# Attention blocks taken two at a time, and the modulation dots spread over fixed steps, in a hybrid encoder step

## The chip, the core and the metric

The kernel runs on one core of a Trainium2 chip. The metric is the device time of one execution in microseconds (us), as a median of several runs. The core has a matrix engine (PE, TensorE, which writes to PSUM banks), VectorE (DVE), ScalarE (ACT), GpSimd (POOL) and SyncE (SP, which here only issues DMA transfers). Each engine works through its own list of instructions in order; they meet at semaphores. Code such as `pe.wait_ge(x, n)` holds PE's list until the semaphore x has reached n.

## What is computed

One layer of a streaming encoder, on 1024 prompt frames and 64 sample frames (T = 1088 tokens in all), in float32. Cut to what matters here:

```python
mod = silu(c) @ w_ada + b_ada                    # shift, scale and gate vectors from the conditioning
h = modulate(rmsnorm(x, ln1), sh1, sc1)
rq, rk, rv, rg, aq, ak, av = split_in(h @ w_in)   # two groups of heads out of one projection
ret_o = retention(rq, rk, rv, rg)                 # 4 heads x 128, a carried state per head
att_o = band_attention(aq, ak, av, sinks)         # 8 query heads, 2 kv heads x 64, window 128, ALiBi, sinks
x = x + g1 * (concat(ret_o, att_o) @ w_out)
h2 = modulate(rmsnorm(x, ln2), sh2, sc2)
x = x + g2 * conv_ffn(h2)                         # gated MLP with a causal convolution of width 3
y = modulate(rmsnorm(x, normf), shf, scf)
```

The attention adds a table of distances and a mask to the scores, takes the row maximum (with the sink), exponentiates, divides by the sum and weighs the values. The retention takes blocks of 128 tokens: scores times a decay table, plus the query times the state carried so far, and a new state.

## The kernel before

**Stages.** A start (normalisation of x and the first three projection units, until about 88 us of the trace), then four "heads" j = 0 to 3 (88 to 450 us), then the output projection, the up projection with the convolution, and the down projection. The change touches the heads alone.

**Units, passes and steps.** Activations lie with features on partitions, tokens along the free axis. A unit is one 128-column tile of `w_in`: it is multiplied with all tokens in three chunks of 364, 362 and 362 columns (PSUM banks 0, 1, 2), and each chunk takes three passes of 8 matmuls (weights and activations are split in a high and a low part). Head j has the units rq, rk, rv, rg and the next head's aq, so 5 x 9 passes; the last head has 4 units and then, in `first_out_unit`, the first unit of the output projection in place of the fifth. After each pass `unit` (line 1922 issues the matmuls) calls `between`, which puts small matmuls for attention and retention in. Pass i of unit p ends in **step** 9p + i: 45 steps a head, with 8 unit matmuls between two steps. A **stretch** s is three steps (3s to 3s + 2); the lists of DVE and ACT are written out by stretches.

**Attention of head j** has 9 query blocks b: 8 of 128 tokens and the last of 64. Four parts on PE and three elsewhere follow one another for a block:
- `scores` (PE, L2006): for both kv groups, keys against queries, into banks 3 and 4; in step 3b.
- `mask_and_max` (DVE, L1460 to L1465): adds the table, takes the maximum, and prepares the exponent's bias, into `prob` and `soft`, which hold two blocks; in stretch b.
- `exps` (ACT, L835, L837), then `normalise` (DVE, L1473 to L1476) in stretch b + 1.
- `transpose_prob` (PE, L2021): four transposes into bank 5, in step 3b + 4; `copy_prob_t` (ACT, L845).
- `weigh_values` (PE, L2036): into bank 6, in step 3b + 6, behind the scores of block b + 2; `copy_att_out` (ACT, L854).

**Retention of head j** has 9 blocks as well. `RET_PE_STEP` gives the PE steps 28, 30, 31, ..., 38. In its k-th entry PE issues `block_scores(k)` (L2051 to L2053, banks 3 or 4) and then `block_output(k - 1)` (L2070 to L2073, banks 6 and 5), which waits for DVE's `take_block(k - 1)` and `next_state(k - 2)`. DVE does `retention(k)` = `take_block(k)` (L1490 to L1492) and `next_state(k - 1)` (L1505) in the stretch that holds the step: k = 0 in stretch 9; 1, 2, 3 in 10; 4, 5, 6 in 11; the rest in 12. In the last head `mix_lo` (L1518) follows most of them on DVE and prepares the low parts for the output projection; POOL does some of these too (L1261).

**Modulation dots.** Each head computes 8 rows of `w_ada` against the conditioning: `ada_dots` (L1352) is two dots of 1024 elements by 128 partitions on DVE, with both operands and the result in SBUF. It waits for a row tile in `ada_w` (two places, so the load of tile i + 2 waits, in SP's list, until the dots of tile i are done). Dots i = 0 to 7 stand at the end of stretches 1 to 8; then `add_ada_bias` (L1358).

**POOL** splits a unit's weights in their low part (L1203, 128 x 1024) when ACT has made the high part (L730), once at the end of each unit. In unit 0 it also scales rq for the retention (`decay_q`, L1227 and L1230), and at the start of a head it finishes the retention output of the head before (`gate_ret`, L1241 and L1244). Ahead of that DVE has three reciprocals (L1559), 7 us together, between two heads.

## Time and profile before

| | |
|---|---|
| median of 3 runs | 1325.32 us (1324.27 to 1325.89) |
| the profiled execution | 1324.34 us, span 1322.5 us |
| busy: PE, weight loads | 1254.9 us (95%), 1182.0 us (89%) |
| busy: DVE, ACT, POOL | 840.2 us (64%), 517.5 us (39%), 520.5 us (39%) |
| mean granted TensorE clock | 0.984 of full speed |
| chain that ended last, by engine | PE 68%, DVE 12%, POOL 6%, issue 5%, DMA 5%, ACT 2% |
| unit matmuls of the heads, L1922 | 1368, 256.5 us busy |

A line of the trace's timeline gives start, duration, engine, source line, operation, result <- operands, and a count where several were merged; in brackets stands idle time of the engine ahead of it, and what ended it. Starts are counted from the start of the span. A matmul's duration overlaps with the next one's; its cost is the distance of two starts. Float32 matmuls are issued in two passes, so that two of them show as x4.

### The profile page before, as it was taken

To read this page: it belongs to the slowest core of one execution; us is meant where nothing else is said; L and a number is where in the kernel's file an instruction comes from. 1 tells how busy PE (TensorE), PEld (TensorE's weight loads), DVE (VectorE), ACT (ScalarE), POOL (GpSimd) and SP (SyncE) were. 2 spreads that over 40 slices of the span, in tenths; PEclk is the share of its full clock that TensorE was granted. 3 is DMA by queue.
4 is the path that set the end of the run, shared out by engine and by line. 5 is a ranking of instruction groups with operands and counts; after the bars stand their busy time and mean duration, and the time that the engine had idled before them with its cause. 6 is when DMAs were issued, how large, how long until landed. Compare 5 with 4: busy or idle time off the path is not lost.

```text
span 1322.5 us, 22445 instructions
## 1 busy us (share of the span) xinstructions
PE 1254.9 (95%) x8537; PEld 1182.0 (89%) x8537; DVE 840.2 (64%) x1503; ACT 517.5 (39%) x1029; POOL 520.5 (39%) x313
## 2 busy tenths in 40 slices
PE   5999999999999999779999999999999999999995
PEld 3568988988989899779999999999999999999995
DVE  6988477396496637995666666666665468663305
ACT  4454345344345513543333333433333323333422
POOL 0012131031232514544353534435352577775760
PEclk9999999999999899899999999999999999999998
DMA  9413032222233412103223232222322898686971
GB/s 363 177 58 125 25 121 79 81 80 87 74 112 103 149 60 99 58 32 132 99 100 115 92 124 99 100 99 100 115 94 83 324 367 289 238 310 213 332 258 46
DMA packets 74392, 185.55 MB, mean 140 GB/s; under 512 B 7424, under 2 KB 39744, under 8 KB 74048
## 3 DMA queue, kind: packets, MB, share of 16 engines
q1 hardware_dynamic: 72640, 183.63, 38.9%
q8 instruction: 59, 0.97, 0.3%
q10 hardware_dynamic: 1664, 0.72, 0.2%
q14 instruction: 29, 0.24, 0.1%
HBM read 150.14 MB, written 34.19 MB: 139 GB/s over the span
## 4 chain that ended last, share of the span: by engine, by line
PE 68%; DVE 12%; POOL 6%; issue 5%; DMA 5%; ACT 2%; SPq 1%; DVEq 0%; ACTq 0%; POOLq 0%
PE bank L2189 33%; PE bank L1922 14%; PE bank L2229 9%; PE bank L2165 5%; DMA w_raw<-in_w_units 3%; POOL w_extra L1315 2%; POOL w_more L1315 2%; PE bank L2036 2%; DVE std L1559 1%; PE bank L2006 1%; PE bank L2021 1%; DVE ada_out L1352 1%; DVE act_hl L1406 1%; POOL w_hl L1315 1%; POOL w_hl L1276 1%
## 5 line engine op out<-in xcount | busy, mean ns | idle before, releaser
L1922 PE MATMUL bank<-act_hl,w_hl 128*128 128x362 f32 (+1 forms) x1368 | 256.5, 336 | 1.3 <-DVE act_hl L1406 1.3
L1922 PEld LDWEIGHTS bank<-act_hl,w_hl 128*128 128x128 f32 x1368 | 223.3, 188 | 10.6 <-issue 8.3
L1203 POOL TENSOR_TENSOR w_hl<-w_raw,w_hl 128x1024 fp32r<-128x1024 f32 x21 | 51.3, 2444 | 332.5 <-ACT w_hl L730 332.5
L2229 PE MATMUL bank<-u_hl,w_more 128*128 128x362 f32 (+1 forms) x672 | 116.3, 332 | 2.6 <-POOL w_more L1315 2.3
L2189 PE MATMUL bank<-x_blocks_a,w_hl 128*128 128x272 f32 x864 | 114.0, 291 | 4.9 <-issue 4.9
L2229 PEld LDWEIGHTS bank<-u_hl,w_more 128*128 128x128 f32 x672 | 113.5, 191 | 3.3 <-POOL w_more L1315 2.6
L2189 PEld LDWEIGHTS bank<-x_blocks_a,w_hl 128*128 128x128 f32 x864 | 111.6, 191 | 5.3 <-issue 5.1
L2189 PE MATMUL bank<-x_blocks_a,w_ext 128*128 128x272 f32 x840 | 110.1, 290 | 4.3 <-DVE prod_sb L1664 2.4
L2189 PE MATMUL bank<-x_blocks_b,w_hl 128*128 128x272 f32 x864 | 112.7, 288 | 1.6 <-ACT x_blocks_b L1013 1.3
L2189 PEld LDWEIGHTS bank<-x_blocks_b,w_hl 128*128 128x128 f32 x864 | 109.8, 188 | 2.4 <-DVE up_b L1669 1.3
L2189 PEld LDWEIGHTS bank<-x_blocks_a,w_ext 128*128 128x128 f32 x840 | 107.5, 190 | 5.0 <-issue 2.6
L2189 PE MATMUL bank<-x_blocks_b,w_ext 128*128 128x272 f32 x840 | 108.3, 287 | 0.0
L2189 PEld LDWEIGHTS bank<-x_blocks_b,w_ext 128*128 128x128 f32 x840 | 106.2, 188 | 0.0
L1315 POOL TENSOR_TENSOR w_more<-w_raw,w_more 128x1024 fp32r<-128x1024 f32 x28 | 76.0, 2734 | 49.6 <-ACT w_more L1103 49.6
L2229 PE MATMUL bank<-u_hl,w_hl 128*128 128x362 f32 (+1 forms) x480 | 83.6, 330 | 3.1 <-POOL w_hl L1315 2.8
L1276 POOL TENSOR_TENSOR w_ext<-w_raw,w_ext 128x512 fp32r<-128x512 f32 x40 | 52.9, 1340 | 83.2 <-ACT w_ext L990 83.2
L1276 POOL TENSOR_TENSOR w_hl<-w_raw,w_hl 128x512 fp32r<-128x512 f32 x40 | 52.3, 1323 | 81.2 <-ACT w_hl L990 81.2
L2229 PEld LDWEIGHTS bank<-u_hl,w_hl 128*128 128x128 f32 x480 | 80.1, 189 | 4.3 <-POOL w_hl L1315 3.4
L2229 PE MATMUL bank<-u_hl,w_extra 128*128 128x362 f32 (+1 forms) x432 | 74.0, 330 | 1.9 <-POOL w_extra L1315 1.9
L2229 PEld LDWEIGHTS bank<-u_hl,w_extra 128*128 128x128 f32 x432 | 72.0, 188 | 3.0 <-POOL w_extra L1315 2.8
L1315 POOL TENSOR_TENSOR w_hl<-w_raw,w_hl 128x1024 fp32r<-128x1024 f32 x20 | 52.8, 2654 | 33.6 <-ACT w_hl L1103 33.6
L2165 PE MATMUL bank<-act_hl,w_hl 128*128 128x272 f32 x480 | 64.1, 297 | 2.0 <-POOL w_hl L1269 2.0
(233 smaller groups left out, 2277.7 us busy)
## 6 DMA issues: line engine op xcount, KB each, us to landing
w_raw<-in_w_units SPq DMA_DIRECT2D x139, 512.0 KB, 4.5
ada_w<-in_w_ada_t SPq DMA_DIRECT2D x36, 512.0 KB, 3.6
u_hl<-u_dram SPq DMA_DIRECT2D x44, 362.0 KB, 5.5
u_dram<-acc SPq DMA_DIRECT2D x22, 544.0 KB, 2.7
u_dram<-up_b SPq DMA_DIRECT2D x22, 544.0 KB, 2.7
ada_d<-in_w_ada_t SPq DMA_DIRECT2D x16, 512.0 KB, 5.7
u_hl<-u_dram SPq DMA_DIRECT2D x22, 364.0 KB, 7.3
xm<-in_x_t SPq DMA_DIRECT2D x2, 1448.0 KB, 13.8
```

What stands on the lines that cost most here:

```text
L1203: pool.tensor_tensor(w_hl[:, slot, 1], w_raw[:, slot], w_hl[:, slot, 0].bitcast(F32), ALU.subtract).then_inc(wl_ready, 1)
L1276: pool.tensor_tensor(w_block(q)[:, 1], a_source(f, i), w_block(q)[:, 0].bitcast(F32), ALU.subtract).then_inc(bl_ready, 1)
L1315: pool.tensor_tensor(w_down(q)[:, 1], w_raw[:, q % 3], w_down(q)[:, 0].bitcast(F32), ALU.subtract).then_inc(dl_ready, 1)
L1352: dve.tensor_tensor_reduce(out, ada_place[place], silu_c[:, s], 1.0, 0.0, ALU.mult, ALU.add, mod_part[:, part, s:s + 1]).then_inc(ada_used, 1)
L1406: dve.tensor_tensor(act_hl[:, 1, k, :], xm[:, k, :], act_hl[:, 0, k, :].bitcast(F32), ALU.subtract).then_inc(lo_ready, 1)
L1559: dve.reciprocal(std[:, c, 0:n], std[:, c, 0:n]).then_inc(inv_ready, 1)
L1922: ins = pe.matmul(bank[c][:, 0:m], w_hl[:, slot, w, k, :], act_hl[:, x, k, a:a + m], start=(pas == 0 and i == 0), stop=(pas == 2 and i == ...
L2006: ins = pe.matmul(bank[3 + g][0:n, 0:kn], aq[h, t:t + n], ak[h, kb[0][0]:kb[0][0] + kn], start=True, stop=True)
L2036: ins = pe.matmul(bank[6][h, 0:n], av_tok[0:k[1], k[3], h], prob_t[0:k[1], r, g, i, 0:n], start=(i == 0), stop=(i == len(kb) - 1))
L2165: ins = pe.matmul(bank[r % 3][:, 0:HC], w_of[:, w, k, :], act_hl[:, x, k, HC * n:HC * n + HC], start=(pas == i == 0), stop=(pas == 2 and i ...
L2189: ins = pe.matmul(n[:, 0:HC], w_block(q)[:, w, P * k:P * (k + 1)], x_half(h)[:, i, x, k, :], start=(first and pas == k == 0), stop=(pas == ...
L2229: ins = pe.matmul(bank[o][:, 0:m], w_down(q)[:, w, o, :], u_hl[:, q % U_RING, x, 0:m], start=(f == pas == 0), stop=(f == FT - 1 and pas == 2))
```

## The change

- Attention's PE parts move to fixed steps, two blocks at a time: scores of (0, 1), (2, 3), (4, 5), (6, 7), (8) in steps 0, 6, 12, 18, 24; transposes in steps 6, 12, 18, 24, 28; values of (0, 1), (2, 3), (4, 5) in steps 12, 18, 24, of (6, 7) in step 28 and of (8) in step 30. Within a step PE issues values, scores, transposes, then retention, in this order.
- The two blocks of a pair use two halves of banks 3, 4 and 6, and banks 5 and 7 for the transposes. `qk_ready` and `pv_ready` are raised once for a pair, by 2. Bank 7 is free when the norm of the head before is done, so the wait for `std_ready` moves from the first values to the first odd transpose.
- DVE masks a pair in stretches 0, 2, 4, 6, 8 and normalises it in stretches 1, 3, 5, 7, 9. The masking of a pair waits for the scores of both blocks.
- The dots stand at the end of stretches 1, 2, 4, 6, 8, 9, 10, 11, behind the retention parts of that stretch; the bias follows the last. ACT's list follows the same tables, values first, then transposes, then exponents.
- Numbers and shapes of all matmuls, DVE, ACT and POOL operations and of all transfers stay as they are.

```diff
--- before.py
+++ after.py
@@ -840,7 +840,7 @@
 
                 qn, r, kb = BLOCKS[b][1], b % 2, keys_of(b)
                 act.wait_ge(pt_ready, NB * j + b + 1)
-                src = bank[5][:, :].rearrange("p (g k q) -> p g k q", g=2, k=2)
+                src = bank[5 + 2 * r][:, :].rearrange("p (g k q) -> p g k q", g=2, k=2)
                 if b < NB - 1:
                     ins = act.activation(prob_t[:, r, :, 0:len(kb), :], src[:, :, 0:len(kb), :], ACT.Copy)
                 else:
@@ -851,7 +851,8 @@
             def copy_att_out(j, b):
                 t, n = BLOCKS[b]
                 act.wait_ge(pv_ready, NB * j + b + 1)
-                act.activation(xm[:, 4 + j, t:t + n], bank[6][:, 0:n], ACT.Copy).then_inc(pv_copied, 1)
+                at = P * (b % 2)
+                act.activation(xm[:, 4 + j, t:t + n], bank[6][:, at:at + n], ACT.Copy).then_inc(pv_copied, 1)
 
             def copy_ret_out(j, b):
                 t, n = BLOCKS[b]
@@ -895,12 +896,13 @@
                         if s == 14:
                             ret_squares(j, (2,))
                             ret_roots(j, (0, 1))
-                        if 2 <= s <= NB + 1:
-                            copy_att_out(j, s - 2)
-                        if s < NB:
-                            exps(j, s)
-                        if 1 <= s <= NB:
-                            copy_prob_t(j, s - 1)
+                        for step in range(3 * s, 3 * s + 3):
+                            for b in ATT_PV_AT.get(step, ()):
+                                copy_att_out(j, b)
+                            for b in ATT_PT_AT.get(step, ()):
+                                copy_prob_t(j, b)
+                            for b in ATT_QK_AT.get(step, ()):
+                                exps(j, b)
                         if mixing and c == 0:
                             split_weights(UNIT_OUT + 1, [UNIT_OUT + 1])
                         for step in (3 * s, 3 * s + 1):
@@ -1457,7 +1459,7 @@
                 dve.wait_ge(qk_ready, NB * j + b + 1)
                 seal_waits(dve)
                 for g in range(2):
-                    ins = dve.tensor_tensor_reduce(prob[0:qn, r, g, 0:kn], bank[3 + g][0:qn, 0:kn],
+                    ins = dve.tensor_tensor_reduce(prob[0:qn, r, g, 0:kn], bank[3 + g][0:qn, 256 * r:256 * r + kn],
                                                    att_tab[0:qn, g, kb[0][2]:kb[0][2] + kn], 1.0, sink_sb[0:qn, g:g + 1],
                                                    ALU.add, ALU.max, soft[0:qn, r, 0, g:g + 1])
                 chain(ins, j)
@@ -1536,19 +1538,20 @@
                         next_state(j, k - 1)
 
                 for s in range(3 * (N_HEAD - last)):
-                    if 1 <= s <= NB:
-                        normalise(j, s - 1)
-                    if s < NB:
-                        mask_and_max(j, s)
-                    if 1 <= s <= 8:
-                        ada_dots(16 + s - 1 + 8 * j, 2 + (s - 1) // 2 + 1 + 4 * j, (s - 1) % 2, s - 1)
-                    if s == NB:
-                        chain(add_ada_bias(16 + 8 * j, 8, 16 + 8 * j + 8), j)
+                    for b in ATT_QK_AT.get(3 * s, ()):
+                        mask_and_max(j, b)
+                    for b in ATT_QK_AT.get(3 * s - 3, ()):
+                        normalise(j, b)
                     for k in range(NB + 1):
                         if RET_PE_STEP[k] // 3 == s:
                             retention(k)
                             if last and k in MIX_LO_AFTER:
                                 mix_lo(*MIX_LO_AFTER[k])
+                    if s in ADA_AT:
+                        i = ADA_AT.index(s)
+                        ada_dots(16 + i + 8 * j, 2 + i // 2 + 1 + 4 * j, i % 2, i)
+                    if s == ADA_AT[-1]:
+                        chain(add_ada_bias(16 + 8 * j, 8, 16 + 8 * j + 8), j)
                 for k in range(7, NB + 1) if last else ():
                     retention(k)
                     mix_lo(*MIX_LO_AFTER[k])
@@ -1997,45 +2000,48 @@
                 if b == 0:
                     pe.wait_ge(av_tok_ready, 3)
                     pe.wait_ge(cache_loaded, 32)
-                else:
+                elif b % 2 == 0:
                     pe.wait_ge(masked_ready, NB * j + b)
                     if b == NB - 1:
                         seal_waits(pe)
+                at = 256 * (b % 2)
                 for g in range(2):
                     h = slice(64 * g, 64 * g + 64)
-                    ins = pe.matmul(bank[3 + g][0:n, 0:kn], aq[h, t:t + n], ak[h, kb[0][0]:kb[0][0] + kn],
+                    ins = pe.matmul(bank[3 + g][0:n, at:at + kn], aq[h, t:t + n], ak[h, kb[0][0]:kb[0][0] + kn],
                                     start=True, stop=True)
-                ins.then_inc(qk_ready, 1)
+                if b % 2 or b == NB - 1:
+                    ins.then_inc(qk_ready, 1 + b % 2)
 
             def transpose_prob(j, b):
                 n, r, kb = BLOCKS[b][1], b % 2, keys_of(b)
                 pe.wait_ge(prob_ready, NB * j + b + 1)
-                if b > 0:
-                    pe.wait_ge(pt_copied, NB * j + b)
+                if b >= 2:
+                    pe.wait_ge(pt_copied, NB * j + b - 1)
+                if b == 1:
+
+                    pe.wait_ge(std_ready, 3 + 3 * j)
                 if b == NB - 1:
                     seal_waits(pe)
                 for g in range(2):
                     at = 0
                     for i, k in enumerate(kb):
                         col = P * (2 * g + i)
-                        ins = pe.transpose(bank[5][0:k[1], col:col + n], prob[0:n, r, g, at:at + k[1]], ident[0:n, 0:n])
+                        ins = pe.transpose(bank[5 + 2 * r][0:k[1], col:col + n], prob[0:n, r, g, at:at + k[1]], ident[0:n, 0:n])
                         at += k[1]
                 ins.then_inc(pt_ready, 1)
 
             def weigh_values(j, b):
                 n, r, kb = BLOCKS[b][1], b % 2, keys_of(b)
                 pe.wait_ge(pt_copied, NB * j + b + 1)
-                if b > 0:
+                if b % 2 == 0 and b > 0:
                     pe.wait_ge(pv_copied, NB * j + b)
-                else:
-
-                    pe.wait_ge(std_ready, 3 + 3 * j)
                 for g in range(2):
                     h = slice(64 * g, 64 * g + 64)
                     for i, k in enumerate(kb):
-                        ins = pe.matmul(bank[6][h, 0:n], av_tok[0:k[1], k[3], h], prob_t[0:k[1], r, g, i, 0:n],
+                        ins = pe.matmul(bank[6][h, P * r:P * r + n], av_tok[0:k[1], k[3], h], prob_t[0:k[1], r, g, i, 0:n],
                                         start=(i == 0), stop=(i == len(kb) - 1))
-                ins.then_inc(pv_ready, 1)
+                if b % 2 or b == NB - 1:
+                    ins.then_inc(pv_ready, 1 + b % 2)
 
             def block_scores(j, b):
 
@@ -2080,13 +2086,12 @@
                 def between(p):
                     def steps(i):
                         s = 9 * p + i
-                        b = s // 3
-                        if s % 3 == 0 and b < NB:
+                        for b in ATT_PV_AT.get(s, ()):
+                            weigh_values(j, b)
+                        for b in ATT_QK_AT.get(s, ()):
                             scores(j, b)
-                        if s % 3 == 1 and 1 <= b <= NB:
-                            transpose_prob(j, b - 1)
-                        if s % 3 == 0 and 2 <= b <= NB + 1:
-                            weigh_values(j, b - 2)
+                        for b in ATT_PT_AT.get(s, ()):
+                            transpose_prob(j, b)
                         if s in RET_PE_STEP:
                             k = RET_PE_STEP.index(s)
                             if k < NB:
@@ -2268,6 +2273,12 @@
 
 MIX_ORDER = [4, 5, 6, 7, 0, 1, 2, 3]
 
+ATT_PV_AT = {12: (0, 1), 18: (2, 3), 24: (4, 5), 28: (6, 7), 30: (8,)}
+ATT_QK_AT = {0: (0, 1), 6: (2, 3), 12: (4, 5), 18: (6, 7), 24: (8,)}
+ATT_PT_AT = {6: (0, 1), 12: (2, 3), 18: (4, 5), 24: (6, 7), 28: (8,)}
+
+ADA_AT = (1, 2, 4, 6, 8, 9, 10, 11)
+
 RET_PE_STEP = [28] + list(range(30, 39))
 
 RET_SUM_STEP = [{41: (0, 1), 43: (2,)}, {40: (0, 1), 42: (2,)}]
```

## Rows read from the trace of the kernel before

**Rows 1.** The page, first part: engine, busy time, share of the span, instructions.

```profile
PE 1254.9 (95%) x8537; PEld 1182.0 (89%) x8537; DVE 840.2 (64%) x1503; ACT 517.5 (39%) x1029; POOL 520.5 (39%) x313
```

**Rows 2.** Chain of waits, a period of three steps in head 1: start, us, what.

```profile
205.36 0.63 PE bank L2006 x4
205.99 0.59 PE bank L2036 x8
206.59 1.53 PE bank L1922 x8
208.11 0.44 PE bank L2021 x4
208.55 2.65 PE bank L1922 x16
```

**Rows 3.** Chain of waits, step 28 of head 1, behind the transposes of block 8.

```profile
231.05 0.26 PE bank L2051
```

**Rows 4.** Timeline of PE: first scores and last transposes of heads 0, 2, 3.

```profile
87.74 0.49 PE L2006 MATMUL bank<-ak,aq 64*128 64x128 f32 x4
140.00 0.45 PE L2021 MATMUL bank<-ident,prob 64*128 64x64 f32 x4
267.34 0.49 PE L2006 MATMUL bank<-ak,aq 64*128 64x128 f32 x4
321.24 0.45 PE L2021 MATMUL bank<-ident,prob 64*128 64x64 f32 x4
357.97 0.49 PE L2006 MATMUL bank<-ak,aq 64*128 64x128 f32 x4
411.30 0.45 PE L2021 MATMUL bank<-ident,prob 64*128 64x64 f32 x4
```

**Rows 5.** Timeline of DVE in head 1: first mask, and one tile's dots.

```profile
179.88 0.25 DVE L1460 CUSTOM_DVE_ANT_0 prob<-bank,att_tab,sink_sb 128x128 f32<-128x128 f32 x1
...
185.62 1.23 DVE L1352 CUSTOM_DVE_ANT_0 ada_out<-ada_w,silu_c 128x1024 bf16<-128x1024 f32 x1
...
188.19 0.16 DVE L1473 TENSOR_TENSOR rden<-soft 128x2 f32<-128x2 f32 x1
```

**Rows 6.** Timeline of DVE and POOL, two places where both work on SBUF.

```profile
193.27 2.74 DVE L1476 TENSOR_SCALAR prob<-prob,rden 128x256 f32<-128x256 f32 x2
193.35 2.51 POOL L1203 TENSOR_TENSOR w_hl<-w_raw,w_hl 128x1024 fp32r<-128x1024 f32 x1 [7.90 <-ACT w_hl L730]
...
376.94 2.41 POOL L1227 TENSOR_TENSOR acc<-rq,rtab 128x1024 f32<-128x1024 f32 x1
376.99 3.43 DVE L1352 CUSTOM_DVE_ANT_0 ada_out<-ada_w,silu_c 128x1024 bf16<-128x1024 f32 x1
```

**Rows 7.** Timeline of all engines around steps 35 to 37 of head 1.

```profile
247.37 0.27 PE L2051 MATMUL bank<-ident,rk 128*128 128x128 f32 x1
...
248.75 0.34 DVE L1505 SCALAR_TENSOR_TENSOR state<-state,rtab,bank 128x128 f32<-128x128 f32 x1
...
250.09 2.38 POOL L1203 TENSOR_TENSOR w_hl<-w_raw,w_hl 128x1024 fp32r<-128x1024 f32 x1 [18.97 <-ACT w_hl L730]
...
250.52 0.35 DVE L1490 TENSOR_SCALAR k_tok<-bank,rtab 128x128 f32<-128x128 f32 x1 [1.44 <-PE bank L2053]
...
252.82 0.49 PE L2070 MATMUL bank<-s_dec,v_tok 128*128 128x128 f32 x2
```

**Rows 8.** Timeline of POOL, DVE and PE in the last head, steps 33 and 34.

```profile
422.71 2.58 POOL L1261 TENSOR_TENSOR act_hl<-xm,act_hl 128x362 fp32r<-128x362 f32 x2 [5.25 <-ACT act_hl L883]
...
424.39 0.34 DVE L1490 TENSOR_SCALAR k_tok<-bank,rtab 128x128 f32<-128x128 f32 x1
...
425.96 0.39 PE L2070 MATMUL bank<-s_dec,v_tok 128*128 128x128 f32 x2
```

**Rows 9.** Windows in the output projection: length, busy of each engine (x instructions), granted clock.

```profile
451.83:458.66 6.83, 6.83 (x47) 6.83 (x46) 1.22 (x3) 4.58 (x8) 6.26 (x3) 0.82 0.56 167
458.66:465.49 6.83, 6.83 (x56) 6.83 (x55) 6.04 (x5) 1.92 (x3) 5.40 (x3) 1.00 0.40 140
```

## The prediction

> **What bounds the kernel now.** I read the page first: PE is busy for 95% of the span [rows 1], so a gain has to come out of PE's own list, and a loss out of waits that are put into it. Then the chain of waits inside a head. In the steady part it lies on PE alone [rows 2]: scores 0.63 us, values 0.59, then 8 unit matmuls in 1.53, transposes 0.44, then 16 unit matmuls in 2.65. Sixteen in 2.65 is 0.166 each, so 8 should take 1.33. The 8 that come back from the values take 0.20 more, the 16 behind the transposes nothing. Attention's small matmuls use half of the array's rows (scores, 64*128) or columns (values, 128*64), the unit and the transposes all of it; the 0.20 is the price of a return to the full array.
>
> Next I compare the heads. From the first scores to the last transposes PE takes 52.26 us in head 0, 53.90 in head 2 and 53.33 in head 3 [rows 4], with the same work; head 1 is like head 2. The excess, 2 x 1.64 + 1.07 = 4.35 us, is PE waiting for DVE, which is still busy with the reciprocals of the head before and masks its first block only 3 us into the head [rows 5].
>
> **Part 1: pairs on PE.** No matmul goes away. Of returns to the full array from scores or values there are ten in a head now (scores in step 0, the eight steps 3 to 24, values in step 27); steps 28 and 30 end in retention. Afterwards only step 0 has one, since every later step ends in transposes or retention. Nine returns x 0.20 x 4 heads = 7.2 us off PE, all on the path. Values followed by scores, and scores followed by transposes, become new transitions, about 8 a head. The nearest row is the first retention transpose behind the half-size ones of block 8, 0.26 [rows 3] against 0.11 (a quarter of 0.44): 0.15 each, 4.8 us if all cost that. On the other side, if second blocks also shed what is lost inside a group (values are 0.59, where four times 0.11 would do), 0.15 x 8 x 4 = 4.8 us more go. So the gain is 2.4 to 12 us; I take 7.2, because the times in rows 2 already contain the change from one half-array shape to another.
>
> The Trainium skill, TensorEngine Tiling (Array Packing), Key Properties, says that a change of tiling mode drains the engine. By that rule only the number of changes counts, three for each block now and three for each pair afterwards, which would put the gain near the upper bound.
>
> **Part 2: waits at the head's start.** DVE starts the first mask at 179.88 [rows 5], 3.2 us behind PE's first scores. Two masks, exponents and two normalisations end about 6.5 us later, at 186.4; the first transposes now come in step 6, some 48 x 0.166 + 1.3 = 9.3 us into the head plus the scores of a pair (1.3), near 187.5. The 4.35 us go.
>
> **Part 3: a normalisation beside POOL.** Normalisation of (2, 3) is queued on DVE behind the dots of tile 1. On ACT the exponents of block 3 precede the split of the unit's weights, so POOL begins its 2.5 us split and the 2.4 + 0.3 us of `decay_q` at about the moment at which the normalisation begins. Rows 6 show what then happens: two L1476, 0.61 us elsewhere, took 2.74 beside the split. Counted through, block 3 is normalised 1.6 us after PE wants its transposes in step 12 (nominally 198.7 in head 1's time). In head 0, with no reciprocals ahead, 0.1. Sum 0.1 + 3 x 1.6 = 4.9 us; the ends are 0 (DVE slips in ahead of POOL) and 7.
>
> **Part 4: dots among the retention.** A tile's dots take 188.19 - 185.62 = 2.57 us of DVE [rows 5]. From step 30 on, PE steps follow each other by 2.44 us (247.37 for step 35), and in each `block_output` waits for DVE's retention part of the step before. What is late:
> - Tile 5, at the end of stretch 9, has the 4.6 us to step 30's retention: nothing, in the last head 0.3.
> - Tile 6, between retention(3) and retention(4): DVE had 1.4 us idle a step and PE needs the state one step later. 2.57 fits but for 0.1 in heads 0 to 2.
> - Tile 7, behind retention(6), whose last operation ends at 249.09 [rows 7]. First dot to about 250.3. POOL's split is ready at 250.09 and takes the SBUF in between, for 2.4 us, to 252.7. The second dot ends at 254.0, the bias at 254.25, then retention(7) needs about 1.0 until the state is written: 255.25. PE's L2070 of step 37 stood at 252.82 and waits for that state: 2.4 us. Nothing else can run on PE, since its unit matmuls are queued behind. Three heads: 3 x (2.4 + 0.1) = 7.5 us. That a dot waits for a whole POOL operation is shown once at full length: 3.43 instead of 1.23, beside L1227 [rows 6].
> - In the last head DVE also has `mix_lo`. Retention(4) starts at 424.39 and ends 1.0 later, 0.6 ahead of PE's 425.96 [rows 8]. Tile 6 comes before it, and waits until 425.3 for POOL's L1261 as well: 0.9 + 2.57 - 0.6 = 2.9 us late. Tile 7 meets the next pair of L1261 in the same way, with the bias on top: 3.1. With tile 5's 0.3 that is 6.3 us; without any POOL wait it would be 4.1.
>
> The skill's page SBUF — State Buffer, Who interferes with whom, says that a DVE instruction with two SBUF inputs and a GpSimd one that reads SBUF exclude each other for the whole instruction, the first one winning. By that rule the second dot of tile 7 is blocked to the end of the split; rows 6 agree. Without it the three heads would lose 0.35 us each instead of 2.5.
>
> **Costed at nothing.** The tile loads are issued later, since each waits for the dots two tiles back, and two unit loads queue behind them on SP; they land some 4 us after issue and are used 10 us or more later, except tile 7 (issued after tile 5's dots, about 12 us ahead). If that cover were gone, a unit's split would be late by the difference. The evacuations that ACT does behind two blocks of exponents have a whole unit (17 us) of slack. The moved `std_ready` wait is satisfied 15 us before.
>
> **Clock.** After PE's waits around 446 to 451 us the granted clock was half (1.2 GHz of 2.4) until about 454: 47 matmuls in 6.83 us against 56 in the next 6.83 [rows 9], 1.1 us lost on the part at half. Five new waits of 2.4 to 3.1 us are nearly as long as those. An estimate: half of them bring a stretch at half clock like that one, 2.5 x 1.1 = 2.7 us; ends 0 and 8.
>
> **The sum**, on the profiled execution of 1324.34 us: - 7.2 - 4.35 + 4.9 + 7.5 + 6.3 + 2.7 = +9.85, so 1334.2 us. The median of before is 1325.32, so against it the change is +8.9 us or 0.7%. The stages behind the heads are taken as unchanged, shifted in time.
>
> **The rivals.**
> - *DVE's SBUF work is not held up* (ends faster). In rows 7, L1490 ran in its usual 0.35 under the split. If dots and normalisations do so as well, Part 3 is 0, tile 7 costs 0.25 and tile 6 0.1 in three heads (1.05), and the last head 4.1. 1324.34 - 11.55 + 1.05 + 4.1 = 1317.9. Against: L1490 reads a PSUM bank, the dots do not. It decides at the second dot of tile 7: if that ends before 252 in head 1's time, this rival holds. 0.12.
> - *PE sheds more than I count*: the upper bound of Part 1 (12) with all waits as forecast, Part 3 nought and no clock loss: 1324.34 - 12 - 4.35 + 7.5 + 6.3 = 1321.8; with one of these at its middle, 1324. 0.16, half of it faster by more than 0.2%.
> - *DVE becomes the bound of the heads*: transitions at 0.15 each (gain 2.4), Part 3 at 7, and clock losses of 8: 1324.34 - 2.4 - 4.35 + 7 + 7.5 + 6.3 + 8 = 1346. For it: DVE is 64% busy and its retention parts sit one step ahead of PE. 0.07.
> - *The change does not do what it says*: waits inside a merged step break the pair up, so that no return is saved, 1341. Since the scores of a step need only masks of the pair before, I see no such wait but that of Part 3. 0.05.
> - The forecast, 1328 to 1341: 0.60.
>
> **How the numbers follow.** About 0.2% (2.7 us) is what a measurement of this kernel can tell from no change. Faster: 0.12 + 0.08 = 0.20. Same (1322.7 to 1328): 0.08 of the second rival and 0.05 at the forecast's lower edge, 0.13. Slower: 0.67. The range leaves out half of the first rival and the outer part of the third: 1319 to 1342.
>
> **What would show it.** Right: in a steady pair step PE's values, scores and transposes take about 3.3 us with no extra in the unit matmuls behind; the first transposes of heads 1 to 3 wait for nothing; an idle PE of 2.4 us ahead of L2070 in step 37 of heads 0 to 2, and a second L1352 of about 3.4 us under L1203; two waits near 3 us in the last head. Wrong: a second dot of 1.23 us in stretch 11, PE waits for `mix_lo` in the last head's output unit, or a new wait for a weight split.

## The result and the profile after

The changed kernel takes 1335.27 us (median of 4 runs, 1332.67 to 1339.13) against 1325.61 us beside it (1324.27 to 1326.34): a ratio of 1.0074, 95% interval 1.0050 to 1.0097. It is slower by 9.7 us. The profiled execution took 1339.13 us with a span of 1337.4. The page's first part, in the columns of [rows 1]:

```profile
PE 1251.9 (94%) x8537; PEld 1190.4 (89%) x8537; DVE 854.2 (64%) x1503; ACT 517.0 (39%) x1029; POOL 522.2 (39%) x313
```

PE is busy 3 us less than in [rows 1] and the span is 15 us longer, so PE waits more. Which engine it waits for is told by the table of PE's waits (line <- releaser: us in total, times, longest). Two groups grew in the heads: `block_output` (L2076), which has no such group before, and the transposes (L2029), which before waited 2.4 us in all, 5 times. The wait of the last head's output unit for `mix_lo` is as before (3.2 us in all against 3.0).

```profile
PE bank L2076 <- DVE state L1507: 11.8, 5, 2.8
PE bank L2029 <- DVE prob L1478: 5.2, 10, 0.8
```

Windows cut at the first scores of each head, with the last one up to the output projection, show where the time goes: length, PE busy, PEld, DVE, ACT, POOL, then the granted clock. First before, then after:

```profile
87.74:176.72 88.98, 88.98 (x593) 79.79 (x592) 54.14 (x161) 37.34 (x102) 15.55 (x7) 1.00 0.25 84
176.72:267.34 90.62, 89.53 (x594) 79.73 (x593) 58.41 (x163) 37.57 (x103) 20.23 (x13) 1.00 0.24 82
267.34:357.97 90.63, 89.53 (x593) 79.74 (x593) 58.40 (x163) 37.57 (x103) 20.23 (x13) 1.00 0.23 82
357.97:451.70 93.73, 89.92 (x585) 79.74 (x585) 71.31 (x185) 47.21 (x127) 33.63 (x26) 0.98 0.33 107
```

```profile
87.34:178.58 91.24, 88.27 (x593) 81.87 (x592) 58.21 (x161) 36.99 (x102) 14.62 (x7) 0.98 0.25 87
178.58:270.73 92.15, 88.38 (x594) 81.92 (x593) 62.85 (x163) 37.59 (x103) 20.16 (x13) 0.98 0.23 80
270.73:363.07 92.34, 88.55 (x594) 82.08 (x593) 62.93 (x163) 37.59 (x103) 20.16 (x13) 0.98 0.23 80
363.07:463.00 99.93, 90.31 (x585) 82.76 (x585) 76.08 (x185) 46.65 (x127) 35.49 (x26) 0.95 0.30 101
```

Heads 0 to 2 are 2.26, 1.53 and 1.71 us longer. The last one, up to the first matmul of the output projection, grew from 93.74 to 100.0 us. In heads 0 to 2 PE is busy about one microsecond less, yet 3 to 4 us of each are now idle, and the clock column is 0.98 where it was 1.00, so the busy time holds some work at a lower clock.

**The gain.** The chain of waits in a steady merged step, which answers to [rows 2]:

```profile
209.69 1.07 PE bank L2041 x16
210.76 1.06 PE bank L2010 x8
211.83 1.02 PE bank L2029 x8
212.85 3.17 PE bank L1925 x19
```

Values, scores and transposes of two blocks take 1.07 + 1.06 + 1.02 = 3.15 us, and the 19 unit matmuls behind them 3.17, 0.167 each, no extra. Before it was 2 x (0.63 + 0.59 + 0.20 + 0.44) = 3.72 [rows 2].

**The loss.** The largest part is in the retention. DVE, POOL and PE in step 37 of head 1, which answers to [rows 7]:

```profile
248.62 1.22 DVE L1354 CUSTOM_DVE_ANT_0 ada_out<-ada_w,silu_c 128x1024 bf16<-128x1024 f32 x1
...
249.71 2.38 POOL L1205 TENSOR_TENSOR w_hl<-w_raw,w_hl 128x1024 fp32r<-128x1024 f32 x1 [19.81 <-ACT w_hl L730]
...
250.04 3.13 DVE L1354 CUSTOM_DVE_ANT_0 ada_w<-ada_w,silu_c 128x1024 f32<-128x1024 f32 x1 [0.19 <-DVE mod_part L1354]
...
254.66 0.74 PE L2076 MATMUL bank<-s_dec,v_tok 128*128 128x128 f32 x2 [2.12 <-DVE state L1507]
```

The second dot of tile 7 takes 3.13 us in place of 1.22 and ends 1.1 us behind POOL's split (249.71 + 2.38 = 252.09). The retention part behind it is late, and PE stands for 2.12 us. Then comes what the windows behind that wait show (same columns as above):

```profile
252.50:254.70 2.20, 0.08 (x2) 0.07 (x1) 1.99 (x8) 0.00 (x0) 0.00 (x0) 1.00 0.00 0
254.70:258.10 3.40, 3.40 (x13) 3.40 (x14) 0.79 (x4) 0.28 (x1) 0.00 (x0) 0.50 0.00 0
258.10:261.50 3.40, 3.40 (x20) 2.92 (x20) 0.35 (x1) 1.61 (x4) 0.00 (x0) 1.00 0.08 22
```

With PE idle for 2.1 us, the granted clock falls to half (1.2 of 2.4 GHz) for the next 3.4 us: 13 matmuls there, 20 in the same length after it. All five long waits of the heads (step 37 in heads 0 to 2, steps 34 and 37 in the last) are followed by such a stretch in this execution. That is not so in every one: see the run with the placement alone.

A smaller part is in the attention. Steps 12 and 28 of head 1, where a normalisation (L1478) meets POOL's split and the transposes behind it wait (in step 12 twice, 0.83 and 0.39 us):

```profile
195.20 2.41 POOL L1205 TENSOR_TENSOR w_hl<-w_raw,w_hl 128x1024 fp32r<-128x1024 f32 x1 [7.85 <-ACT w_hl L730]
195.59 4.53 DVE L1478 TENSOR_SCALAR prob<-prob,rden 128x256 f32<-128x256 f32 x2
...
200.17 0.66 PE L2029 MATMUL bank<-ident,prob 128*128 128x128 f32 x4 [0.83 <-DVE prob L1478]
...
227.30 2.71 DVE L1478 TENSOR_SCALAR prob<-prob,rden 64x192 f32<-64x192 f32 x2
...
230.16 0.42 PE L2029 MATMUL bank<-ident,prob 64*128 64x64 f32 x4 [0.43 <-DVE prob L1478]
```

### The profile page after: what moved, and what is told of

Its sections match the earlier page's. It is cut to its first block, busy times and chain, and to the rows that moved or that the text cites. A ratio compares the mean times of both kernels' runs of the same rounds, so it can differ in the third digit from the quotient of the medians.

```text
span 1337.4 us, 22424 instructions
## 1 busy us (share of the span) xinstructions
PE 1251.9 (94%) x8537; PEld 1190.4 (89%) x8537; DVE 854.2 (64%) x1503; ACT 517.0 (39%) x1029; POOL 522.2 (39%) x313
## 4 chain that ended last, share of the span: by engine, by line
PE 64%; DVE 16%; issue 7%; POOL 5%; DMA 4%; ACT 2%; SPq 2%; DVEq 0%; ACTq 0%; POOLq 0%
PE bank L2194 32%; PE bank L2234 11%; PE bank L1925 10%; PE bank L2170 5%; DMA w_raw<-in_w_units 2%; DVE prob L1478 2%; DVE ada_out L1354 2%; POOL w_extra L1317 1%; DVE std L1562 1%; PE bank L2041 1%; DVE prob L1462 1%; PE bank L2029 1%; POOL w_hl L1317 1%; POOL w_hl L1278 1%; DMA ada_d<-in_w_ada_t 1%
## 5 line engine op out<-in xcount | busy, mean ns | idle before, releaser
L1925 PE MATMUL bank<-act_hl,w_hl 128*128 128x362 f32 (+1 forms) x1368 | 246.4, 336 | 1.1 <-POOL w_hl L1205 1.1
L1925 PEld LDWEIGHTS bank<-act_hl,w_hl 128*128 128x128 f32 x1368 | 228.3, 191 | 4.4 <-issue 2.7
L1205 POOL TENSOR_TENSOR w_hl<-w_raw,w_hl 128x1024 fp32r<-128x1024 f32 x21 | 54.4, 2591 | 334.7 <-ACT w_hl L730 334.7
L1317 POOL TENSOR_TENSOR w_hl<-w_raw,w_hl 128x1024 fp32r<-128x1024 f32 x20 | 52.7, 2648 | 36.0 <-ACT w_hl L1105 36.0
```

Of the source, the lines that this page charges most:

```text
L1205: pool.tensor_tensor(w_hl[:, slot, 1], w_raw[:, slot], w_hl[:, slot, 0].bitcast(F32), ALU.subtract).then_inc(wl_ready, 1)
L1317: pool.tensor_tensor(w_down(q)[:, 1], w_raw[:, q % 3], w_down(q)[:, 0].bitcast(F32), ALU.subtract).then_inc(dl_ready, 1)
L1925: ins = pe.matmul(bank[c][:, 0:m], w_hl[:, slot, w, k, :], act_hl[:, x, k, a:a + m], start=(pas == 0 and i == 0), stop=(pas == 2 and i == ...
```

## The experiments

The theory: the pairs on PE are a gain of about 14 us with the heads' starts, and everything lost comes from where the dots stand, by three mechanisms: the dots' own length, DVE's stop behind POOL's work in SBUF, and the half clock behind PE's long waits. The rivals: the loss comes with the pairs; POOL only happens to run beside the dots; the half clock has another cause.

**Dots put back to stretches 1 to 8.**

```diff
-ADA_AT = (1, 2, 4, 6, 8, 9, 10, 11)
+ADA_AT = (1, 2, 3, 4, 5, 6, 7, 8)
```

> The changed kernel with the dots of a head put back to the ends of stretches 1 to 8; the attention in pairs stays. It tells the two halves of the change apart. Theory (the loss is made by the dots that stand among the retention, and the pairs alone are a gain): the waits of 2.2 us in step 37 of heads 0 to 2 and of 2.7 and 2.9 us in the last head go, and so do the stretches at half clock behind them; what stays is the wait of step 12 (0.6 + 1.45 + 1.5 + 1.25 = 4.7 us) and the 0.46 us of step 28. By the traces: 1325.3 - 9.6 (pairs) - 4.35 (heads' start) + 4.7 + 1.4 = 1317.4; counted from the changed kernel's 1335.3 it would be 1314. So 1314 to 1318. Rival (most of the loss comes with the pairs, as more waits in the merged steps): 1326 or more.

Measured: 1321.26 us, ratio to before 0.9966 (0.9956 to 0.9977). The change's sign flips with the dots alone, so the rival falls; but the time is 3 us above the expected range. PE's waits in L2076 are gone. In their place there is one of 1.30, 1.30 and 1.35 us in step 28 of heads 0 to 2 (0.51 in the last), which the expectation had at 0.46. Head 1:

```profile
225.77 2.37 POOL L1205 TENSOR_TENSOR w_hl<-w_raw,w_hl 128x1024 fp32r<-128x1024 f32 x1 [15.81 <-ACT w_hl L730]
226.06 2.11 DVE L1360 TENSOR_TENSOR mod<-mod_part,b_ada_sb 128x16 f32 x1 [0.17 <-DVE mod_part L1354]
...
228.59 0.54 DVE L1478 TENSOR_SCALAR prob<-prob,rden 64x192 f32<-64x192 f32 x2
229.28 0.42 PE L2029 MATMUL bank<-ident,prob 64*128 64x64 f32 x4 [1.30 <-DVE prob L1478]
```

The bias (L1360) follows the last tile, and it met POOL's split: 2.11 us for an operation of 16 columns that takes 0.17 elsewhere. The normalisation behind it was late. The four waits of step 28 are 4.5 us in place of the 1.4 expected, which is 3.1 of the 3.9 us that the time lies above the sum.

**Last tile out of stretch 11.**

```diff
-ADA_AT = (1, 2, 4, 6, 8, 9, 10, 11)
+ADA_AT = (1, 2, 4, 5, 6, 8, 9, 10)
```

> The changed kernel, dots at the ends of stretches 1, 2, 4, 5, 6, 8, 9, 10: no tile in stretch 11 any more. Theory: in heads 0 to 2 the 2.2 us wait of step 37 goes with its stretch at half clock (about 1.7 us each), and in the last head the wait of step 37 (2.9 us and its 1.7); the wait of step 34 of the last head stays at 2.7. 1335.3 - 3 x 3.9 - 4.6 = 1319. Rival (the clock falls have another cause and stay): 1335.3 - 3 x 2.2 - 2.9 = 1325.8. Rival (the wait only moves to the step behind the tile, now in stretch 10, since DVE is full there too): 1333 to 1336.

Measured: 1322.11 us (ratio 0.9974, 0.9964 to 0.9984), 13.2 us below the changed kernel, where 16 were expected. Heads 0 to 2 took 87.64, 88.52 and 88.54 us, which is 3.6 to 3.8 less than in the changed kernel, where 3.9 were expected; the last head came down by 4.0, to 96.0. That makes 15.0 us in the profiles, of the 16.3 that the expectation adds up to. In the medians another 1.8 are missing; the sizes had been read from the changed kernel's profiled run, which was its slowest. The rival in which the clock falls stay (1325.8) is 3.7 us too high, and the granted clock of heads 0 and 1 is 1.00; the one in which the wait only moves is out: tile 7 costs 0.29 us in stretch 10.

**POOL's split cut short.**

```diff
-pool.tensor_tensor(w_hl[:, slot, 1], w_raw[:, slot], w_hl[:, slot, 0].bitcast(F32),
+pool.tensor_tensor(w_hl[:, slot, 1, 0:kt], w_raw[:, slot, 0:kt], w_hl[:, slot, 0, 0:kt].bitcast(F32),
...
-split_weights(head_unit(j, p) + 2, [head_unit(0, p) + 2])
+split_weights(head_unit(j, p) + 2, [head_unit(0, p) + 2], 1 if p in (2, 3) else KT)
```

> The changed kernel, but in heads 0 to 2 POOL's subtraction that makes the low part of the weights covers only the first 128 of its 1024 columns for two of the five units of a head (those whose split falls beside step 28 and beside step 37); the rest of these low parts is left out of the computation. DVE's, ACT's and PE's lists are as they were. Theory (the second dot of tile 7 and the normalisation of block 8 wait for the end of the split in SBUF): the second dot falls from 3.1 to 1.25 us, the wait of step 37 from 2.2 to about 0.3 us, the 0.46 us of step 28 go, and with them the half clock behind step 37: 1335.3 - 3 x (1.9 + 0.46 + 1.7) = 1323. The last head stays. Rival (DVE is late by the length of its own work, POOL only happens to run beside it): both waits and the time stay, 1334 to 1336. If the waits go but not the half clock: 1328.

Measured: 1327.06 us (ratio to before 1.0006, 0.9993 to 1.0019). Not one instruction of DVE or PE differs from the changed kernel, and the same place of head 1 now reads:

```profile
245.39 0.45 POOL L1205 TENSOR_TENSOR w_hl<-w_raw,w_hl 128x128 fp32r<-128x128 f32 x1 [21.25 <-ACT w_hl L730]
...
245.72 1.22 DVE L1354 CUSTOM_DVE_ANT_0 ada_w<-ada_w,silu_c 128x1024 f32<-128x1024 f32 x1 [0.19 <-DVE mod_part L1354]
...
248.44 0.46 PE L2076 MATMUL bank<-s_dec,v_tok 128*128 128x128 f32 x2 [0.25 <-DVE state L1507]
```

The dot is back at 1.22 us, the wait at 0.25, and step 28 waits for nothing. Heads 0 to 2 shrink by 3.9 us each (91.24, 92.15, 92.34 to 87.35, 88.28, 88.43), where 4.06 was forecast; the last head stays at 100.0. POOL is the cause, and the dots' own length leaves 0.25 us of 2.1. The median is 4 us above the expected 1323, though the heads of the profiles show the full 11.7 us: as in the run above, the sizes were read in the slowest run of the changed kernel and taken off its median.

**Waits filled with matmuls.**

```diff
+last = isinstance(j, int)
+if b == 7 or last and b == 4:
+    ...
+    for i in range(14 if last else 11):
+        k = ks[i % len(ks)]
+        pe.matmul(bank[7][:, 0:362], w_hl[:, slot, 0, k, :], act_hl[:, 0, k, lo:lo + 362],
+                  start=True, stop=True)
 pe.matmul(bank[6][:, 0:n], v_tok[0:n, r, :], s_dec[0:n, r, 0:n], start=True, stop=(b == 0))
```

> The changed kernel, with matmuls whose result nobody reads, into the free bank 7, ahead of the waiting block_output: 11 in step 37 of heads 0 to 2, 14 in steps 34 and 37 of the last head, 362 columns each. They fill most of PE's waits, which stay as long as they are. Theory (the half clock follows PE's idle time): the waits end when they did, but no half clock comes behind them: 5 x up to 1.7 us, 1335.3 - 5 to 8 = 1327 to 1330. Rival (the half clock comes from elsewhere, or returns as much as was saved): 1334 to 1337. If the fillers are longer than the waits, by their excess more.

Measured: 1329.77 us, 5.5 us less than the changed kernel, with 61 matmuls more. PE in head 1, and the windows of the filler and of the stretch behind it:

```profile
251.28 2.08 PE L2072 MATMUL bank<-act_hl,w_hl 128*128 128x362 f32 x11
...
253.47 0.46 PE L2084 MATMUL bank<-s_dec,v_tok 128*128 128x128 f32 x2
```

```profile
251.28:253.40 2.12, 2.08 (x13) 1.77 (x11) 1.91 (x8) 0.00 (x0) 0.00 (x0) 1.00 0.00 0
253.40:256.80 3.40, 3.33 (x21) 2.87 (x21) 0.90 (x4) 0.75 (x2) 0.00 (x0) 1.00 0.00 0
```

The output matmul of step 37 starts as late as before, and the clock behind it is 1.00 with 21 matmuls in 3.4 us; so it is behind all five filled waits. The mean granted clock of the ten runs is 0.985 to 0.987, where the four of the changed kernel have 0.980 to 0.984: where PE's idle time is filled, the half clock stays away. Heads 0 to 2 lose 1.43, 1.35 and 1.61 us, the last one 3.0 for its two waits: one stretch at half clock costs 1.5 us, five of them 7.4 in the profiles, 5.5 by the medians.

**The placement alone, on the kernel before** (in DVE's list of before, the last three lines of the loop over stretches as in the changed kernel; nothing else).

> The kernel before, with nothing changed but the place of the dots: ends of stretches 1, 2, 4, 6, 8, 9, 10, 11, behind the retention parts. Attention stays block by block. With the run that put the dots back, it tells whether the two halves of the change add up. Theory: the waits of steps 34 and 37 come as in the changed kernel, with their half clock: 3 x (0.1 + 2.2 + 1.7) + 2.7 + 2.9 + 3.4 = +21, less up to 2 us of the waits at the heads' start, as stretch 3 has no dots: 1344. The clock lost 2 to 3 us less in timed runs than in the profiled one, so 1340 to 1345. Rival (the waits need the pairs, which put two normalisations and two masks in a stretch): 1325 to 1330.

Measured: 1343.58 us (ratio 1.0140, 1.0118 to 1.0163), within the range of the theory. The waits do not need the pairs: PE stands for 2.16, 2.12 and 2.12 us in step 37 of heads 0 to 2 and for 2.55 and 2.87 in the last. The two halves add up: -10.2 and -4.35 us from pairs and heads' starts, +4.5 and +1.4 from the two waits that only pairs bring (steps 12 and 28; the sizes are in the table below) make -8.7, and from this run to the changed kernel it is 1335.27 - 1343.58 = -8.3.

The half clock, however, is not as the theory had it. Behind four of the five waits the granted clock stayed at 1.00 in the profiled execution. Head 0, the same place as in head 1 of the changed kernel:

```profile
164.25 0.46 PE L2071 MATMUL bank<-s_dec,v_tok 128*128 128x128 f32 x2 [2.16 <-DVE state L1505]
...
164.91 1.58 PE L1923 MATMUL bank<-act_hl,w_hl 128*128 128x364 f32 x8
```

The 8 unit matmuls take 1.58 us; in head 1 of the changed kernel, behind a wait of 2.12 us, they take 2.57. Only head 2 shows half clock, from 351.1 to 358.1 us, and is 3.0 us longer than head 1. So a wait of 2.1 to 2.9 us can bring half clock and need not; what decides it, these runs don't show. That the time was met all the same is luck in part: the waits at the heads' start did not shrink as forecast (0.70 to 0.92 us where 0.69 was), and 2.5 us of the profiled execution arose behind the heads.

**Dots between.**

```diff
 for b in ATT_QK_AT.get(3 * s - 3, ()):
     normalise(j, b)
+if s == 9:
+    ada_dots(16 + 6 + 8 * j, 2 + 3 + 1 + 4 * j, 0, 6)
...
-i = ADA_AT.index(s)
+i = (0, 1, 2, 3, 4, 5, 7)[ADA_AT.index(s)]
...
-ADA_AT = (1, 2, 4, 6, 8, 9, 10, 11)
+ADA_AT = (1, 3, 4, 5, 6, 7, 9)
```

> A version meant to keep the pairs' gain without the waits: attention in pairs as in the changed kernel; dots of tile 0 at the end of stretch 1, none in 2, tiles 1 to 5 at the ends of 3 to 7, none in 8, tile 6 in stretch 9 between the normalisation of block 8 and the first retention part, tile 7 at the end of stretch 9. Theory: with no dots in stretch 2 the normalisation of (2, 3) starts ahead of POOL's split, so the wait of step 12 goes; with none in 8 the normalisation of block 8 is in time; stretches 10 and 11 have retention alone. 1325.3 - 9.6 - 4.35 = 1311.4, range 1310 to 1314. Rival (two tiles in stretch 9 make the first retention part late): a wait ahead of step 30 of up to 2 us in each head, 1315 to 1319.

Measured: 1311.52 us (1309.93 to 1313.23), ratio to before 0.9891 (0.9877 to 0.9906). It beats both kernels, at the expected 1311.4. Its heads:

```profile
87.75:174.18 86.43, 86.43 (x594) 80.38 (x593) 54.24 (x161) 36.90 (x102) 17.21 (x7) 1.00 0.26 87
174.18:260.64 86.46, 86.46 (x594) 80.42 (x593) 61.07 (x163) 37.39 (x103) 21.70 (x13) 1.00 0.25 86
260.64:347.10 86.46, 86.46 (x594) 80.42 (x593) 61.08 (x163) 37.38 (x103) 21.71 (x13) 1.00 0.25 86
```

PE is never idle in three heads, and their clock column is 1.00. The rival's wait for the first retention part shows in the last head alone, 0.74 us. Yet the collision with POOL is still there; nobody waits behind it (head 1):

```profile
221.77 2.37 POOL L1205 TENSOR_TENSOR w_hl<-w_raw,w_hl 128x1024 fp32r<-128x1024 f32 x1 [15.28 <-ACT w_hl L730]
221.87 3.36 DVE L1354 CUSTOM_DVE_ANT_0 ada_w<-ada_w,silu_c 128x1024 f32<-128x1024 f32 x1 [0.19 <-DVE mod_part L1354]
225.16 0.34 DVE L1492 TENSOR_SCALAR k_tok<-bank,rtab 128x128 f32<-128x128 f32 x1
```

**One tile in stretch 8 in place of the middle of 9.** The edit: the two added lines go, and `ADA_AT = (1, 3, 4, 5, 6, 7, 8, 9)`.

> As the version with the dots between, but tile 6 at the end of stretch 8 in place of the middle of stretch 9 (stretch 2 stays empty, tile 7 stays at the end of 9). It tells which of the two moves removed which wait. Theory: the wait of step 12 stays away, since it hung on the dots in stretch 2; the wait of step 28 comes back, since the normalisation of block 8 then stands behind two sets of dots and starts beside POOL's split: 1.3 us in a head, as in the run with the dots early: 1311.5 + 4 x 1.3 = 1316.7. Rival (the wait of step 28 hangs on the sum of the dots up to there, which is 7 tiles here and 8 in that run): 1311 to 1313.

Measured: 1314.31 us (1312.53 to 1317.03), between the two expectations. Step 12 waits for nothing, step 28 for 0.66, 0.49 and 0.48 us in heads 0 to 2, which the rival did not have. That the place of each tile counts, and not how many came before, is shown by two other runs: the changed kernel has five tiles ahead of that normalisation and a wait of 0.43 us, the run with the dots between has six and no wait. But 0.5 us is not 1.3: here the bias stands in stretch 9, out of the way, and the normalisation itself meets the split (2.66 us at 222.40 in head 1, where POOL starts at 222.52). The forecast had carried the 1.3 over without it.

**Transposes first, and values and scores interleaved.** Both on the version with the dots between, where no wait disturbs PE.

```diff
+for b in ATT_PT_AT.get(s, ()) if s < 28 else ():
+    transpose_prob(j, b)
 for b in ATT_PV_AT.get(s, ()):
     weigh_values(j, b)
 for b in ATT_QK_AT.get(s, ()):
     scores(j, b)
```

> As the version with the dots between (run beside it), but in steps 6, 12, 18 and 24 PE issues transposes, then values, then scores, so that the unit follows half-size matmuls. The number of changes of shape in a step stays the same; what changes is that 4 steps a head end in half-size matmuls in place of transposes. By the prediction's step (0.20 us for a return to the unit from half-size matmuls, nothing from transposes): 4 x 4 x 0.20 = +3.2 us against the version beside it. Rival (every change of shape costs the same, wherever it stands): 0, within 0.5 us.

Measured: 1312.32 us against 1311.52, +0.8 in place of +3.2. The runs of the two versions overlap (1311.13 to 1313.57, 1309.93 to 1313.23), so 0.8 is hardly told from nothing, but well from 3.2. The chain of waits in step 18 of head 1:

```profile
203.97 0.87 PE bank L2031 x8
204.84 1.07 PE bank L2043 x16
205.92 1.06 PE bank L2012 x8
206.98 1.03 PE bank L1927 x5
```

Five unit matmuls take 1.03 behind the scores, 0.20 more than 5 x 0.166, as in [rows 2]. But the transposes cost 0.87 where they cost 1.02 behind scores. The return from half-size matmuls is paid either way: 0.20 at the unit, or 0.15 at the transposes. This step is 0.05 us longer in all. In step 6 of heads 1 to 3 there was 0.2 to 0.3 us more, with a gap between the transposes of the two blocks: they stand 1.1 us earlier in this order, and in head 1 DVE's normalisation of block 1 ends at 183.02, just ahead of its transposes at 183.15. In head 0, where it ends 3 us earlier, step 6 is 0.02 us longer.

```diff
+for i in range(2):
+    for b in ATT_PV_AT.get(s, ())[i:i + 1]:
+        weigh_values(j, b)
+    for b in ATT_QK_AT.get(s, ())[i:i + 1]:
+        scores(j, b)
```

> As the version with the dots between (run beside it), but in steps 12, 18 and 24 values and scores alternate (values b, scores b', values b + 1, scores b' + 1), which puts two more changes of shape in each of these steps, 24 in all; between half-size shapes only. Theory A (a change between two half-size shapes costs as much as a return to the full array, 0.20 us): +4.8 us against the version beside it. Theory B (only the return to the full array costs): +0 to 0.5 us.

Measured: 1314.94 us, +3.4. The same step:

```profile
204.83 0.59 PE bank L2043 x8
205.42 0.63 PE bank L2012 x4
206.06 0.59 PE bank L2043 x8
206.65 0.63 PE bank L2012 x4
207.28 1.02 PE bank L2031 x8
```

3.46 us in place of 3.15, for the same 32 matmuls: two more changes of shape cost 0.31 us, 0.155 each. So it is theory A, with a price three quarters as large. The expectation also counted one change too many a head: in step 24 there is only block 8 to score, which makes one more change and 0.11 us more (2.67 in place of 2.56). That is 5 a head, 20 in all, and 0.70 us longer heads 1 and 2 in the profiles. The blocks now cost exactly what they cost one by one (0.59 and 0.63, [rows 2]).

## Why the prediction was right, and where it was not

The predicted 1334.2 us stands against 1335.3. The sum, in the order of its terms; "found" is from the traces.

| term | forecast | found | from |
|---|---|---|---|
| pairs on PE | -7.2 | -10.2 | head 0, 88.98 to 86.43 with the dots between, x 4 |
| heads' starts | -4.35 | -4.35 | heads 1 and 2 no longer than head 0 (86.46, 86.43) |
| step 12 | +4.9 | +4.5 | 0.46 + 1.36 + 1.53 + 1.15: how much later PE is in step 18 of each head than with the dots between |
| step 28 | 0 | +1.4 | 0.46 in heads 0 to 2 |
| tiles 5 and 6 in the first three heads | +0.3 | +0.3 | 0.1 a head |
| tile 7 | +7.2 | +6.4 | 2.1 a head |
| last head | +6.3 | +5.4 | 2.55 + 2.84 |
| half clock | +2.7 | +7.4 (5.5 by medians) | run with the filled waits |
| sum | +9.85 | +10.9 (9.0) | |

The output projection starts at 463.08 in place of 451.71, 11.4 us later, though the heads began 0.4 us earlier; of the 11.8 us by which the heads are longer the terms explain 10.9. By the medians the change is +9.7, and the terms make 9.0. The other 3.4 us of the profiled run arose behind the heads, where nothing was changed; the timed runs of this kernel spread over 6 us, and I put nothing on them.

**What held.** Part 3 (a normalisation beside POOL) and tile 7 are the mechanism of the forecast to the operation: the second dot takes 3.13 us against 3.4 forecast, and the run with the short split takes POOL's share away. The rival "DVE's SBUF work is not held up" is refuted by it. The Trainium skill, SBUF — State Buffer, Who interferes with whom, names this as an exclusive lock between a DVE instruction with two SBUF inputs and a GpSimd instruction that reads SBUF; the traces agree for the dots (3.13 us beside POOL, 1.22 without) and for the bias (2.11 against 0.17), and show it for L1478 too, whose operands are a tile and a column of scalars (4.53 us for two that take 0.62).

**Part 1 was mis-sized, by 3.0 us, because its step was wrong.** It booked the 0.20 as a price of coming back to the unit and let transitions inside a step go free. The last two runs show a price at every kind of change that they moved: 0.20 us into the unit from half-size matmuls, 0.15 into transposes, 0.155 between values and scores (0.11 for the one change added in step 24). Counted so, a steady pair has 6 changes before (into scores, into values, back, twice) and 3 after: 3 x 0.155 to 0.20 covers the 0.57 us measured (3.72 to 3.15). Over a whole head, each entry into a shape and each return counted, it is 31 changes before and 18 after; 13 x 0.155 to 0.20 are 2.0 to 2.6 us, against 2.55 measured in head 0. That the forecast was no farther off is partly luck: in a pair it missed a cost (the change into transposes, +0.15) as well as a gain (entry and middle of the second block, -0.31). The nearest row for the missing price stood in the text, 0.26 against 0.11 [rows 3], and was kept as a bound only. The Trainium skill, TensorEngine Tiling (Array Packing), Key Properties, says that a change of the tiling mode drains the engine. The prediction had noted that by this rule the gain would be near the upper bound of 12; the measured 10.2 us lie between that and the 7.2 that I took, and the runs agree that it is the changes that cost.

**The clock was mis-sized, by 4.7 us in the profile and 2.8 by the medians.** The guess was that half of the five waits bring a half-clock stretch, at 1.1 us each. In the profiled execution all five did, the shortest behind 2.1 us of idle PE, at 1.5 us each. How many do is not fixed by the length of the wait: in the run with the placement alone it was one of five, and the 5.5 us by the medians would be between three and four of them (5.5 / 1.5, an estimate). The 1.1 came from [rows 9], whose first window holds only a part of such a stretch: a mean clock of 0.82 over 6.83 us is 2.5 us at half (0.18 x 2 x 6.83), where the new stretches last 3.4. The half clock had begun before that window: in the trace of before the windows 447.40:449.98 and 449.98:453.40 read 0.51 and 0.50.

**Step 28 was missed.** Part 3 followed the normalisation of (2, 3) against POOL and did not ask the same of block 8, which stands behind tile 4's dots in the same way: its L1478 took 2.71 us beside the split, and PE waited 0.43. Twice in this case an expectation took a wait without asking what stood ahead of it in DVE's list (the bias was the other).

**The last head** was late as forecast in steps 34 and 37, at 2.55 and 2.84 us; of tile 5's 0.3 the trace shows nothing, PE waits at no step between 12 and 34 there.

The errors have opposite signs (-3.0, -0.4, -0.8 and -0.9 against +1.4 and, by the medians, +2.8), so the closeness of 1.1 us is in good part luck. The sign owes less to it: with the found terms and no half clock at all the sum is still +3.5, and each half was seen alone, the placement 18 us above before, the pairs without the waits 14 below.

## What to carry to other kernels

- Take matmuls of one shape together: here a change of array shape cost 0.11 to 0.20 us, and 18 of them a head in place of 31 gave 2.5 us a head, 10.2 in all. Look for the price in rows at every change, not only where the long matmuls resume.
- Before work that could stand anywhere goes into an engine's list, ask who waits behind it, and what runs on POOL at that moment. A DVE operation of 1.2 us that meets a POOL operation of 2.4 us is one of 3.1 to 3.4 us. The same collision cost nothing one step ahead of the retention and 3.6 us a head inside it.
- Price a wait of PE with what may follow it: 2.1 us of idle PE cost 3.6 in the changed kernel, of which 1.5 came afterwards, as half clock. Give that part a range from nothing to all waits, since it was there behind five of five in one execution and behind one of five in another.

## What the runs showed of the hardware

- Waits of PE of 2.1 to 2.8 us were followed by a stretch of 3.4 us at 1.2 GHz in all of five cases of the changed kernel, but behind only one of five waits of 2.1 to 2.9 us in the run with the placement alone, where it lasted 7.0 us; with the wait filled by 11 matmuls nobody reads, the clock stayed at 2.4 GHz and the head became 1.4 us shorter. In the run with the dots early the waits of heads 0 to 2 are 1.35 us and shorter, and the granted clock of these heads is 1.00.
- A DVE operation of 128 x 16 elements (0.17 us) took 2.11 us because it began 0.29 us behind POOL's split: the stop is about as long as what is left of POOL's operation, for this small operation as for the dots of 1024 columns.
- The retention operation that reads a PSUM bank (L1490 of before) was not stopped beside POOL: 0.35 us under the split in [rows 7], as elsewhere.
